# Hybrid decoder layer: attention heads fed with activations that are not yet normalized

## The reference

```python
h = rms_norm(h_res, norm_mix_g[l])          # x * rsqrt(mean(x*x) + eps) * g
dq, dk, dv, fq, fk, fv, f_logit, g_a, g_b = split_cols(h @ w_in[l], W_IN_SPLITS)
dq = partial_rope(rms_norm(dq.reshape(...), diff_q_norm_g[l]), cos, sin)   # dk too
fq = rms_norm(fq.reshape(...), fox_q_norm_g[l])                            # fk too
log_f = jax.nn.log_sigmoid((f_logit + b_forget[l]).astype(jnp.float32))
merged = (jax.nn.sigmoid(g_a + b_gate[l, 0]) * y_diff
          + jax.nn.sigmoid(g_b + b_gate[l, 1]) * y_fox)
```

## Time and profile before

| what | value |
|---|---|
| median of three runs | 2038.46 us (2034.68 to 2041.88) |
| profiled execution, its time | 2040.84 us |
| profiled execution, its span | 2039.0 us |
| TensorE busy | 1976.9 us, 97% |
| VectorE busy | 1654.5 us, 81% |
| ScalarE busy | 1141.4 us, 56% |
| GpSimd busy | 685.3 us, 34% |

### The profile page before, as it was taken

How to read it: one execution, slowest core, us unless ns; L and a number is a source line. 1 busy time by engine, 2 the same in 40 slices (tenths; PEclk the granted TensorE clock), 3 DMA queues, 4 the chain that set the end, 5 groups by cost and what they waited for, 6 DMA issues and landing times. The chain is left out here.

```text
span 2039.0 us, 32470 instructions
## 1 busy us (share of the span) xinstructions
PE 1976.9 (97%) x11640; PEld 1746.3 (86%) x11640; DVE 1654.5 (81%) x2318; ACT 1141.4 (56%) x1636; POOL 685.3 (34%) x352
## 2 busy tenths in 40 slices
PE   5999999999999998999999999999999999999998
PEld 4999889998988887999999999999777777777776
DVE  6765676567777657999999999988788888888886
ACT  5655566656577445566656565654455555555554
POOL 2000000000000000688888888888222222222220
PEclk9999999999999998999999999999999999999999
DMA  5556545565545554899998999999899999999997
GB/s 182 186 185 195 189 159 179 184 197 170 177 149 192 175 169 161 299 327 323 324 328 308 320 328 331 350 363 353 297 389 373 366 376 365 387 370 385 371 376 231
DMA packets 137568, 565.28 MB, mean 277 GB/s; under 512 B 44240, under 2 KB 52304, under 8 KB 88112
## 3 DMA queue, kind: packets, MB, share of 16 engines
q1 hardware_dynamic: 87456, 415.36, 57.0%
q0 software_dynamic: 49920, 147.33, 21.3%
q10 hardware_dynamic: 144, 2.10, 0.2%
HBM read 547.18 MB, written 16.88 MB: 277 GB/s over the span
## 5 line engine op out<-in xcount | busy, mean ns | idle before, releaser
L428 DVE TENSOR_TENSOR wlo<-raw,whi 128x1024 fp32r<-128x1024 f32 x242 | 293.8, 1223 | 165.2 <-PE psum L554 109.5
L748 PE MATMUL psum<-xr,whi 128*128 128x384 f32 x2048 | 381.8, 337 | 0.1
L550 PE MATMUL psum<-xr,whi 128*128 128x512 f32 x1408 | 366.3, 402 | 9.9 <-DVE xr L1359 5.3
L769 PE MATMUL psum<-whi,xr 128*128 128x512 f32 x1536 | 371.3, 391 | 4.6 <-ACT xr L1050 3.5
L748 PEld LDWEIGHTS psum<-xr,whi 128*128 128x128 f32 x2048 | 352.2, 189 | 0.5 <-ACT whi L434 0.3
L769 PEld LDWEIGHTS psum<-whi,xr 128*128 128x128 f32 x1536 | 289.1, 188 | 67.7 <-ACT xr L1050 3.7
L434 ACT ACTIVATE whi<-raw 128x2048 fp32r<-128x2048 f32 x169 | 322.6, 1909 | 24.3 <-DMA raw<-v_rows 16.4
L550 PEld LDWEIGHTS psum<-xr,whi 128*128 128x128 f32 x1408 | 255.5, 190 | 61.0 <-issue 7.7
L1095 POOL DMA_INDIRECT arena<-v_rows,small x64 | 138.5, 2163 | 406.2 <-DVE arena L1442 405.6
L421 ACT ACTIVATE whi<-raw 128x1024 fp32r<-128x1024 f32 x244 | 248.8, 1053 | 34.7 <-PE psum L554 17.8
L1100 POOL DMA_INDIRECT gates<-small x96 | 215.8, 2248 | 29.3 <-issue 29.3
(11 more groups left out here) (241 smaller groups left out, 3093.9 us busy)
## 6 DMA issues: line engine op xcount, KB each, us to landing
raw<-stream SPq DMA_DIRECT2D x244, 512.0 KB, 3.4
raw<-v_rows SPq DMA_DIRECT2D x85, 1024.0 KB, 7.6
raw<-u_cols SPq DMA_DIRECT2D x84, 1024.0 KB, 6.6
arena<-v_rows SPq DMA_DIRECT2D x43, 1024.0 KB, 7.6
arena<-u_cols SPq DMA_DIRECT2D x42, 1024.0 KB, 6.1
gates<-arena POOLq DMA_DIRECT2D x8, 1536.0 KB, 9.5
small<-gates SPq DMA_DIRECT2D x62, 192.0 KB, 8.1
arena<-x_t SPq DMA_DIRECT2D x4, 544.0 KB, 6.6
```

The costliest lines, as they stand in the source:

```text
L428: nc.vector.tensor_tensor(wlo[:, k % 2 * HALF:(k % 2 + 1) * HALF], raw[:, s * HALF:(s + 1) * HALF], f(whi[:, s * HALF:(s + 1) * HALF]), AL ...
L550: mm(bank(b), whi[:, s * HALF + c * P:s * HALF + (c + 1) * P], both[c], start=start and c == 0, stop=False)
L748: mm(bank(at, 0, 2 * TD), hi_w[:, c * P:(c + 1) * P], z_all[:, :, c, 0:TD // TS, :], start=c == 0, stop=False)
L769: last = mm(at[:, (b * 4 + j * 2 + n) * 512:(b * 4 + j * 2 + n + 1) * 512], weights, src, start=begin, stop=end, skip_group_check=True)
```

## The change

The heads read x times the norm weight; `rstd0` is multiplied onto the products.

- Start: ScalarE makes `xhi` from the raw activations with the norm weight as scale, chunk by chunk, with the squares in between; VectorE makes `xlo` from the same; the squares are added in pairs of chunks, so that TensorE multiplies eight of them for the mean, behind the forget logits. The forget logits are multiplied by `rstd0` and get their bias on VectorE, which was a bias operand on ScalarE.
- Loop: for the wide blocks VectorE multiplies the bank by `rstd0` into SBUF, and ScalarE waits for that (`wide_scaled`), where it copied from the bank; for the others VectorE adds the halves and then multiplies by `rstd0`. The gates' bias moves into the Sigmoid.
- Loads: the norm and forget weights get a small load of their own behind the first quarter of x; the first weight halves come between the quarters; constants and other parameters later.

```diff
+            act.wait_ge(few_loaded, 16)
+            x_hi(0)
+            A(wf_hi, C["w_forget"], ACT.Copy).then_inc(wf_split, 1)
+            x_square(0)
+            x_hi(1)
+            x_square(1)
+            x_hi(2)
+            x_square(2)
             hi_half(act, 0, 0)
+            x_hi(3)
+            x_square(3)
+            hi_half(act, 0, 1)
             act.wait_ge(first_loaded, 16)
             A(scal[:, 8:9], C["eps"], ACT.Sqrt)
             act.wait_ge(ms_done, 1)
             A(rstd0, bank(7, 0, L), ACT.Sqrt, bias=eps).then_inc(std_done, 1)
...
@@ TensorE, behind the forget logits
+            pe.wait_ge(first_loaded, 16)
+            for k in range(8):
+                pe.wait_ge(sums_done, k // 2 + 1)
+                last = mm(bank(7, 0, L), C["mean2048"], hn[:, k // 2 * 4 + k % 2, :], start=k == 0, stop=k == 7)
+            last.then_inc(ms_done, 1)
...
@@ ScalarE, loop over the heads
-                    elif p < 4:
-                        at, n = QK_AT[names[p]]
-                        A(qk_raw[:, at:at + n], bank(p % 2, 0, n), ACT.Copy)
-                        A(qk_sq[:, at:at + n], bank(p % 2, 0, n), ACT.Square).then_inc(bank_free, 1)
                     elif p < 6:
-                        A(vT[p - 4], bank(p % 2, 0, L), ACT.Copy).then_inc(bank_free, 1)
+                        act.wait_ge(wide_scaled, i * len(WIDES) + (WIDES.index(p) + 1))
+                        if p < 4:
+                            at, n = QK_AT[names[p]]
+                            A(qk_sq[:, at:at + n], qk_raw[:, at:at + n], ACT.Square).then_inc(bank_free, 1)
+                        else:
+                            act.nop().then_inc(bank_free, 1)
...
@@ VectorE, in front of the loop
+            dve.wait_ge(std_done, 1)
+            ch.link(V.reciprocal(rstd0, rstd0))
             z, a_, e_, l_ = (fg[n][0:HEADS, :] for n in range(4))
-            dve.wait_ge(forget_z, 1)
+            dve.wait_ge(forget_ps, 1)
+            ch.link(V.tensor_tensor(z, psum[0:HEADS, 6 * 512:6 * 512 + L], rstd0[0:HEADS, :], ALU.mult))
+            ch.link(V.tensor_scalar(z, z, C["b_forget"][0:HEADS, :], None, ALU.add))
...
@@ VectorE, loop over the heads, behind lo_half of step (p, j)
+                        if j and p in WIDES:
+                            into = qk_raw[:, QK_AT["dk" if p == 1 else "fk"][0]:][:, 0:L] if p < 4 else vT[p - 4]
+                            V.tensor_tensor(into, bank(p % 2, 0, L), rstd0, ALU.mult).then_inc(wide_scaled, 1)
                         if j and p in PAIRS:
...
-                            V.tensor_tensor(into, bank(p % 2, 0, T), into, ALU.add).then_inc(low_added, 1)
+                            ch.link(V.tensor_tensor(into, bank(p % 2, 0, T), into, ALU.add))
+                            V.tensor_tensor(into, into, rstd0[:, META:], ALU.mult).then_inc(low_added, 1)
```

More of the change, by code:

```diff
@@ L231, in hybrid_layer @@
         lam_t = w0.take(64)
-        sums = [small[:, n * L:(n + 1) * L] for n in range(4)]
         wf_hi, wf_lo = (whi[:, 3 * HALF + n * P:3 * HALF + (n + 1) * P] for n in range(2))
@@ L443, in _, with load_x @@
         def _(sp):
[L444 to L448, removed]
+            def load_x(c):
+                sp.dma_start(xT[:, 4 * c:4 * c + 4, :].rearrange("p k t -> p (k t)"),
+                             x_t[:, 4 * c * L:(4 * c + 4) * L]).then_inc(x_loaded[c], 16)
+            load_x(0)
+            sp.dma_start(p_sb[:, 0:FIRST_PARAMS], params[:, 0:FIRST_PARAMS]).then_inc(few_loaded, 16)
+            load_x(1)
             def load(h, s):
@@ L452, in load @@
                              ).then_inc(landed[s], 16)
[L454 to L458, removed]
+            load_x(2)
+            load(0, 0)
+            load_x(3)
+            load(1, 1)
+            sp.dma_start(c_sb[:, 0:FIRST_CONSTS], consts[:, 0:FIRST_CONSTS]).then_inc(first_loaded, 16)
+            load(2, 2)
+            sp.dma_start(p_sb[:, FIRST_PARAMS:], params[:, FIRST_PARAMS:]).then_inc(params_loaded, 16)
             sp.dma_start(c_sb[:, FIRST_CONSTS:], consts[:, FIRST_CONSTS:]).then_inc(loaded, 16)
+            load(3, 3)
             with sp.Fori(0, F_U // 2 - 1) as i:
@@ L575, in mul_block @@
                 mul_half(base, k + 1, acc, hi[8:16], lo[8:16], False, True, second)
[L578 to L582, removed]
             pe.wait_ge(wf_rest, 1)
@@ L808, in _, with x_hi, x_square @@
             eps = C["eps"]
-            for k in range(0, KC, 4):
-                act.wait_ge(x_loaded[k // 4], 16)
-                A(hn[:, k:k + 4, :], xT[:, k:k + 4, :], ACT.Square).then_inc(sq_done, 1)
+            def x_hi(c):
+                act.wait_ge(x_loaded[c], 16)
+                for k in range(4 * c, 4 * c + 4):
+                    last = A(xhi[:, k, :], xT[:, k, :], ACT.Copy, scale=C["g_mix"][:, k:k + 1])
+                    if k + 1 in [b for _, b in PIECES]:
+                        last.then_inc(split_hi, 1)
+            def x_square(c):
+                A(hn[:, 4 * c:4 * c + 4, :], xT[:, 4 * c:4 * c + 4, :], ACT.Square).then_inc(sq_done, 1)
+            act.wait_ge(few_loaded, 16)
[6 more added lines that the diff above has]
+            x_square(2)
             hi_half(act, 0, 0)
+            x_hi(3)
+            x_square(3)
+            hi_half(act, 0, 1)
             act.wait_ge(first_loaded, 16)
@@ L849, in _ @@
                         A(qk_raw[:, at:at + n], bank(p % 2, T, T), ACT.Copy).then_inc(low_copied, 1)
[L850 to L853 removed]
                     elif p < 6:
[L855 removed]
+                        act.wait_ge(wide_scaled, i * len(WIDES) + (WIDES.index(p) + 1))
[4 more added lines that the diff above has]
+                            act.nop().then_inc(bank_free, 1)
                     else:
                         g = i * 4 + (p - 6)
[L858 to L859 removed]
+                        A(gates[:, ds(g, 1), :].rearrange("p a t -> p (a t)"), bank(p % 2, T, T),
+                          ACT.Copy).then_inc(low_copied, 1)
                     if p == 9:
@@ L921, in sigmoids @@
             def sigmoids(i, q):
-                gs = [gates[:, ds(i * 2 + q + KC * n, 1), :].rearrange("p a t -> p (a t)") for n in range(2)]
-                A(gs[0], gs[0], ACT.Sigmoid)
-                A(gs[1], gs[1], ACT.Sigmoid).then_inc(sig_done, 1)
+                for n in range(2):
+                    g = gates[:, ds(i * 2 + q + KC * n, 1), :].rearrange("p a t -> p (a t)")
+                    last = A(g, g, ACT.Sigmoid, bias=C["b_gate"][:, ds(i * 2 + q + KC * n, 1)])
+                last.then_inc(sig_done, 1)
             def branch_low(i, m):
```

51 lines of the change are left out of this document (17 added, 34 removed).

## The result

The changed kernel takes 2064.25 us (median of 6 runs, 2061.92 to 2065.85); the kernel before, run beside it, 2040.17. The ratio is 1.012, interval 1.0107 to 1.0133: 24.1 us slower, where 19.1 was forecast. Both parts went the way they were read, the start earlier and the head loop longer, and both were some us worse than worked out.

A forecast was written before the change was run, and what follows sets the result against it. TensorE alone was taken to pace the head loop, with no slack in the ScalarE-VectorE chain to the scores. Start -4.2 plus eight heads at 2.91 (+23.3) gave +19.1 on 2038.46: 2057.6 us, called 2058; range 2045 to 2068.

The forecast's parts named there:

- The period of a head is set by the order of ScalarE and VectorE, not by their busy time: Head loop: both engines are free by busy time, but their program order costs 2.91 us per head.
- Block 4's wait, +1.41: Head loop: ScalarE waits for VectorE's product, delaying rotation copies, rope sum and TensorE's scores by 1.41 us per head.
- Block 5's chain, +0.1 and +1.4: Head loop: ScalarE waits for a product behind a Reciprocal; head norm costs 0.1 us, late probabilities 1.4 us per head.
- Block 3, "nothing": Head loop: ScalarE waits some 3.4 us for the Reciprocal but is back before block 4 needs it; no cost.
- The stream starts 8.6 earlier, the first low product 5.7: Start: weight stream at 23.6 instead of 32.24, first wide low product at 35.9 instead of 41.66.
- The clock behind the gap of 4.6, 1.5: Start: TensorE idles 4.6 us before the first wide low product, then runs at lowered clock, costing 1.5 us.
- Near the one of 1.63 that left its clock alone: Head loop: TensorE's gaps of 1.75 and 1.35 us are near a start gap that did not lower its clock.
- rival (3): Start brings nothing because TensorE is slow there, each head costs 3.4 us; +28.2, 2067 us; chance 0.14.
- Rival (4): Head loop: each head also pays the uncovered table load's 1.28 us a second time; +29.3, 2068 us; chance 0.03.
- (1): Head loop: only the wait before the scores grows, block 5's chain having unseen slack; +7.9, 2046.4 us; chance 0.12.
- (2): Head loop stays paced by TensorE, so only the start counts; 2034.3 us, or 2030; chance 0.11.

The follow-up runs named there:

- product_first: Changed kernel with VectorE's product of a wide block ahead of the weight-half split in the same step instead of behind it; 2042.63 us, ratio 1.0013.
- v5_by_scalar: Changed kernel with block 5's bank copied by ScalarE as before, without the token factor, block 4 as changed; 2053.97 us, ratio 1.007.
- v_at_transpose: Changed kernel with v of blocks 4 and 5 copied by ScalarE, the token factor applied at the copy of the transposed v; 2042.76 us, ratio 1.0018.
- the kernel named both: v_at_transpose with lambda's dot products and Exp moved earlier and a spare-column operation bringing the first table load under the first DMA; 2035.97 us, ratio 0.9983.
- lambda_first: Changed kernel with lambda's dot products ahead of VectorE's first splits and its Exp ahead of the mean's root; 2056.54 us, ratio 1.0079.
- loop_only: Kernel before with the change's three head-loop edits and the old start; 2064.66 us, ratio 1.0128.
- loads_as_before: Changed kernel with loads in nearly the order of before, keeping the small load for norm and forget weights; 2065.37 us, ratio 1.0126.

## Why the prediction was right, point by point

- **The period of a head is set by the order of ScalarE and VectorE, not by their busy time.** Right, and shown by product_first, which changes the order alone.
- **Block 4's wait, +1.41.** Measured +1.55. The hand-over from VectorE's product to ScalarE's weight halves was put at 0.03; it took 0.19 (275.92 to 276.11). An instruction that only raises `bank_free` stands between; behind block 1's product, where ScalarE goes on with a Square at once, it took 0.04 in the same head. That this instruction is the cause is argued, not tested.
- **Block 5's chain, +0.1 and +1.4.** Measured 0.12 and 1.47, together 1.59. v5_by_scalar, without it, is shorter by 69.83 - 68.29 = 1.54.
- **Block 3, "nothing".** True for the sum, since block 4's wait covers it; wrong as a statement on slack. ScalarE is back 0.57 after it is wanted, as v_at_transpose shows. In the prediction's own numbers, "back at 265.3" stood beside a copy that began at 264.63, and "before block 4 needs it" was true only of a block 4 that is itself late.
- **The stream starts 8.6 earlier, the first low product 5.7.** 8.2 and 4.8. The step that was short is ScalarE's start at 4.9: the table load of 1.28, of which the earlier trace rows shows no sign, came when the first quarter had landed, and the first copy began at 5.87. In the kernel named both, where the load runs at 0.76 again, the first copy begins at 4.84. The copies took the 0.41 or so that was put for them (four between 5.87 and 7.54).
- **The clock behind the gap of 4.6, 1.5.** The mechanism was right; the term measured 2.74 in this execution. It was taken from a gap of 3.35 where half clock showed for one group of eight products, some 3.3 us; here it holds for some 6.1, to about 42.9. One number is too little for this term: in the seven kernels with this gap it came out anywhere from 1.52 (v5_by_scalar, product_first) to 2.74, so the 1.5 is its lower end.
- **"Near the one of 1.63 that left its clock alone."** Wrong for the wait before the scores: behind 1.9 the granted clock fell in three of seven heads looked at, which takes TensorE 1.40 each time. It changed the sum by nothing, since the wait for the probabilities gave it back. That was luck: the prediction had not named this cover, and v5_by_scalar shows the price without it.
- **No late transfer in the loop.** Not foreseen: 2.3 in head 0 of the profiled execution, in some profiles only.

The measured time lies inside the range. In the profiled execution the start misses by 2.1, the period by 8 x 0.22 = 1.8, head 0 by 2.3, all to the slow side: 6.2, where the medians are 5.0 off. The result is a little beyond the 2052 to 2064 called likeliest, and by the time alone its 24.1 is nearer to rival (3)'s 28.2 than to the 19.1 of the forecast; only the rows tell the two apart. Rival (4), which the prediction says its range leaves out, has 2067.8 by its own sum and lies just inside it. Of the rivals, (1) and (2) fell with the second wait and with the first; (3) has its mechanism in part, a TensorE slow at the start, but behind the gap and not in the mean (sixteen instructions in 3.83, as forecast); the start still brings 2.1, and a head costs 3.13 and not 3.4. (4) fell: the Exp load at 291.73 took 1.28 and the next operation began at 293.03, so the drain that the Trainium skill (ScalarE: Activation LUTs, What ACT_TABLE_LOAD costs) puts on top of it shows in no row of this case: not here, where the load is in the open, and not at 33.89 in the earlier trace rows.

## What to carry to other kernels

Before work is moved to an engine with idle time, look at what stands ahead of it in that engine's program and at who waits behind the result: here ten operations of 0.4 us cost 3.1 us a head, and exchanging two neighbours gave 2.4 of it back. A factor of a row or column has several places where it can be applied; the one where it is a scale of a copy that is made anyway costs no hand-over. And when a wait is taken away, ask which shorter one it covered: two of these experiments stopped at 0.9 where 0.34 was expected, for the wait of block 3, which the prediction had listed and put at nothing.

## What the runs showed that was not expected

- Ahead of an operation with one wait the table load ran before the data were there: at 0.76 in the kernel before, the data landing at 4.63, and at 274.26 in the earlier trace rows, 3.5 before the scores for it. In the changed kernel two waits stand ahead of the first copy, and the load came at 4.58, with the data. Whether it stands between the two waits or behind both, the rows don't show. An operation on a spare column, ahead of the waits for loads, was in the kernels with the low product at 32.0 to 32.1; lambda_first, without it, has 33.20.
- TensorE's clock behind an idle gap, by the granted clock in the stretches behind it: 0.50 behind 4.87 (1.52 to 2.74 us lost, by kernel) and behind the earlier trace rows's 3.35; behind 1.9 either full or lowered, to 0.60 over a stretch of three us in head 2, for 1.40 to 1.56 us; full behind the waits of 0.34, 0.68 and 0.91 in all eight heads of the kernel before, product_first and v_at_transpose.
- Where the gap of 1.9 lowers the clock, it does so in every other head: heads 2, 4 and 6 of the changed kernel (and head 0, behind its 3.38), heads 0, 2, 4 and 6 of loop_only and lambda_first, heads 1, 3, 5 and 7 of loads_as_before. These four have heads of 69.8 to 70.0 us. In v5_by_scalar, with heads of 68.3 and the same gap, it is head 0 alone. So the length of the gap doesn't decide it by itself; what else does was not settled.
